# Early expert loads into regions that the mixers have left, and two modulation groups summed on VectorE, in a two-layer diffusion backbone

## What is computed

```python
# modulation: per layer six vectors, for the latent and the context stream
mod = silu(c) @ w_mod[l] + b_mod[l]            # w_mod (2, 1024, 6144)
# sub-layer 1: three token mixers, merged
y = g_a * (a @ w_br_mla) + g_b * (b @ w_br_na) + g_m * (m @ w_br_ml)
y = y @ w_out                                  # g_* = sigmoid of three 1024-wide slices of h @ w_in
# sub-layer 2: each of 16 experts takes its 32 best tokens of each stream
hid = silu(xs @ w1[e]) * (xs @ w3[e])          # w1, w3, w2: (2, 16, 1024, 1024)
y = (hid @ w2[e]) * g[e]                       # scattered back and added
```

## Time and profile before

| | us |
|---|---|
| median of 3 executions | 2017.98 |
| lowest, highest | 2014.64, 2026.0 |
| the profiled execution | 2019.38 |
| its span, first to last instruction | 2017.6 |
| TensorE busy (share of the span) | 1724.3 (85%) |
| VectorE busy | 456.9 (23%) |
| ScalarE busy | 325.8 (16%) |
| expert loads: 384 of 1 MB, median from issue to landing | 17.9 |
| mean granted clock of TensorE | 0.933 |

### The profile page before, as it was taken

One profiled execution on the slowest core, in us unless ns is written; L12 is line 12 of the kernel. 1 busy time (PEld: TensorE's weight loads), 2 busy tenths in 40 slices (PEclk: granted clock), 3 DMA queues, 4 the chain that ended last, 5 costly groups with the idle time before them and its releaser, 6 DMA issues.

```text
span 2017.6 us, 21841 instructions
## 1 busy us (share of the span) xinstructions
PE 1724.3 (85%) x9307; PEld 884.3 (44%) x9307; DVE 456.9 (23%) x990; ACT 325.8 (16%) x776; POOL 93.3 (5%) x168
## 2 busy tenths in 40 slices
PE   6999999999998998979888799999996666676665
PEld 2656354444476332424222376767873323222221
DVE  2045144211113112112120514253112101011102
ACT  4113243100023100101000311242021000000001
POOL 5000110000012000000000000110000000000000
PEclk9999999999999999999999899999997778777777
DMA  9310104545416999999999922114635999999995
GB/s 348 101 42 21 16 1 188 196 159 187 147 65 238 403 421 422 421 421 421 421 421 421 389 85 63 16 32 157 209 126 241 421 421 421 421 420 421 421 421 247
DMA packets 130668, 525.18 MB, mean 260 GB/s; under 512 B 9886, under 2 KB 73532, under 8 KB 75276
## 3 DMA queue, kind: packets, MB, share of 16 engines
q1 hardware_dynamic: 127884, 520.47, 65.3%
q0 software_dynamic: 2688, 3.32, 0.9%
HBM read 522.70 MB, written 1.05 MB: 260 GB/s over the span
## 4 chain that ended last, share of the span: by engine, by line
PE 57%; DMA 37%; DVE 4%; ACT 1%; issue 1%; SPq 0%; DVEq 0%; ACTq 0%
DMA ring<-in_w_e_dram 36%; PE ps L690 13%; PE ps L950 9%; PE ps L1127 6%; PE ps L956 4%; PE ps L986 4%; PE ps L914 3%; PE ps L876 2%; PE ps L619 2%; PE ps L1081 2%; PE ps L1149 2%; PE ps L792 2%; PE ps L1107 2%; PE ps L625 1%; DMA ring<-in_w_mod_dram 1%; PE ps L898 1%
## 5 line engine op out<-in xcount | busy, mean ns | idle before, releaser
L1127 PE MATMUL ps<-ring,arena 128*32 128x256 f32 (+1 forms) x3072 | 409.2, 512 | 129.4 <-DMA ring<-in_w_e_dram 126.5
L1127 PEld LDWEIGHTS ps<-ring,arena 128*32 128x32 f32 (+1 forms) x3072 | 131.7, 130 | 391.6 <-DMA ring<-in_w_e_dram 213.1
L1149 PE MATMUL ps<-ring,arena 128*32 128x256 f32 (+1 forms) x1536 | 221.5, 560 | 84.6 <-DMA ring<-in_w_e_dram 80.8
L950 PE MATMUL ps<-arena,ring 128*128 128x512 f32 (+1 forms) x576 | 192.4, 487 | 0.0
L690 PE MATMUL ps<-arena,ring 128*128 128x512 f32 (+1 forms) x480 | 176.9, 527 | 1.4 <-DVE arena L1671 1.4
L1149 PEld LDWEIGHTS ps<-ring,arena 128*32 128x32 f32 (+1 forms) x1536 | 70.5, 140 | 231.4 <-issue 114.7
L1495 ACT ACTIVATE arena<-ps 128x512 f32<-128x512 f32 (+1 forms) x32 | 15.7, 490 | 815.6 <-PE ps L1127 815.6
L950 PEld LDWEIGHTS ps<-arena,ring 128*128 128x128 f32 x576 | 108.7, 190 | 77.9 <-issue 70.4
L1890 DVE COPY arena<-ps 32x512 f32<-32x512 f32 (+1 forms) x128 | 70.8, 553 | 284.1 <-PE ps L1149 282.8
L690 PEld LDWEIGHTS ps<-arena,ring 128*128 128x128 f32 x480 | 90.8, 191 | 83.6 <-issue 77.7
L1195 ACT ACTIVATE arena<-ps 128x512 f32<-128x512 f32 (+4 forms) x162 | 78.4, 489 | 210.9 <-PE ps L986 65.8
(11 more groups left out here) (200 smaller groups left out, 1309.5 us busy)
## 6 DMA issues: line engine op xcount, KB each, us to landing
ring<-in_w_e_dram SPq DMA_DIRECT2D x384, 1024.0 KB, 17.9
ring<-in_w_mod_dram SPq DMA_DIRECT2D x48, 1024.0 KB, 9.2
ring<-in_w_in_dram SPq DMA_DIRECT2D x44, 1024.0 KB, 10.1
ring<-in_w_out_dram SPq DMA_DIRECT2D x8, 1024.0 KB, 10.2
arena<-in_w_br_ml_dram SPq DMA_DIRECT2D x8, 512.0 KB, 6.4
arena<-in_w_br_mla_dram SPq DMA_DIRECT2D x8, 256.0 KB, 3.8
arena<-in_w_br_na_dram SPq DMA_DIRECT2D x8, 256.0 KB, 4.7
arena<-in_rpb_dram POOLq DMA_DIRECT2D x16, 96.0 KB, 4.1
```

The source lines that it names most:

```text
L950: mm = pe.matmul(ps[:, u % 3, tq], wg[:, k, cols], hT[:, k, tq], start=k == 0, stop=k == KD - 1)
L1127: mm = pe.matmul(ps[M * j:M * j + M, m, 0:NW], XST[e // GROUP % 2][:, kk, e % GROUP, 0:M], w[:, k, j * NW:(j + 1) * NW], start=kk == 0, st ...
L1149: mm = pe.matmul(ps[M * j:M * j + M, 3, 0:NW], lhs, w[:, k, j * NW:(j + 1) * NW], start=kk == 0, stop=kk == KD - 1)
```

## The change

What it does:

- **Early expert loads.** `SPARE` names, by the place of a load in the expert order (from 0), loads that go to a region outside the ring. In layer 0 these are loads 0 to 3, into `mix0` to `mix3`, which are the first 8192 columns of the arena (the projections' input and the mixers' outputs). In layer 1 they are 0 (the rows of the context in `X`), 1 (`mixer_consts`: masks, rope table and a projection, now in one tensor), 2 (the first branch buffer), 7 to 10 (`mix0` to `mix3`) and 11 (the second half of `merged`). Each region has a condition that SP waits for (`spare_free`). Every region is used once in a layer; all other loads take the ring's slots in turn, and each waits for the load that had its slot before (`PREVIOUS`).
- **Order of issue.** In layer 0 SP issues expert loads 0 to 3 ahead of the last four modulation loads of group 4; in layer 1 expert loads 0 and 1 ahead of the four output weights.
- **Modulation.** In layer 0 group 1 is computed on TensorE in the first six units (three, three and two products). Groups 2 and 3 are summed on VectorE: after each unit from u = 6 and from u = 15, for eight units, `mod_part` takes one load and adds it, times the column of silu(c), to two sums of 128 x 2048 (`mod_acc`, one for each stream). TensorE sums these over the partitions at u = 14 and u = 23 (8 matmuls each, with `pick`, a column of ones), and releases the slots of these loads in order with its own, in each odd unit, ahead of the last two branch matmuls.
- **What had to move for it.** The gate rows of group 2 are spread in the round e = 14 in place of 1. Scratch areas for squares, the transposed rows, the gathered rows and the gates get other addresses; in layer 1 the memset of `Ya` covers the latent half.

The diff, cut to its core:

```diff
@@ -109,15 +108,18 @@
-def mod_steps(step):
-    n = 3 * KD
-    return range(n * step // MERGE_STEPS, n * (step + 1) // MERGE_STEPS)
-def mod_step(o):
-    return next(s for s in range(MERGE_STEPS) if o * KD - 1 in mod_steps(s))
+def mods_first(l, step):
+    return [(1, k) for k in range(3 * step, min(3 * step + 3, KD))] if l == 0 and step < 3 else []
+SUMMED = {2: 6, 3: 15}
+def mods_summed(l, u):
+    return [(o, u - first) for o, first in SUMMED.items() if l == 0 and first <= u < first + KD]
...
@@ -132,8 +134,10 @@
                 loads += [("in", layer, C_BG + m * D + jp * BLK, BLK)]
-            if layer == 0:
-                loads += [("mod", *MOD_GROUPS[1 + n // KD], n % KD) for n in mod_steps(3 * jp + m)]
+            step = 3 * jp + m
+            for u in (2 * step - 1, 2 * step):
+                loads += [("mod", *MOD_GROUPS[o], k) for o, k in mods_summed(layer, u)]
+            loads += [("mod", *MOD_GROUPS[o], k) for o, k in mods_first(layer, step)]
         if 1 <= jp < KD // 2 - 1:
...
@@ -192,6 +196,42 @@
+SPARE = [{0: "mix0", 1: "mix1", 2: "mix2", 3: "mix3"},
+         {0: "ctx_rows", 1: "mixer_consts", 2: "branch0", 7: "mix0", 8: "mix1", 9: "mix2", 10: "mix3", 11: "merged_end"}]
+SLOT_OF, PREVIOUS, USE = [], [], []
+def _assign_slots():
+    turn, last, count = 0, {}, {}
+    for l in range(2):
+        spare = [None] * len(ring_loads(l)) + [SPARE[l].get(j) for j in range(len(EXPERT_LOADS))]
+        for name in spare:
+            slot = name
+            if name is None:
+                slot, turn = turn % SLOTS, turn + 1
+            count[slot] = count.get(slot, 0) + 1
+            PREVIOUS.append(last.get(slot))
+            last[slot] = len(SLOT_OF)
+            SLOT_OF.append(slot)
+            USE.append(count[slot])
+_assign_slots()
+def issue_order(l):
+    order = [(w, None) for w in weight_loads(l)]
+    experts = [(("expert", l, *a), j) for j, a in enumerate(EXPERT_LOADS)]
+    if l == 0:
+        return order[:-4] + experts[:4] + order[-4:] + experts[4:]
+    return order[:-4] + experts[:2] + order[-4:] + experts[2:]
...
@@ -222,12 +262,13 @@
-        mask_f = sb("mask_f", 512)
-        mask_b = sb("mask_b", 640)
-        rope_t = sb("rope_t", 2, SEQ)
+        mixer_consts = sb("mixer_consts", 2176)
+        mask_f = mixer_consts[:, 0:512]
+        mask_b = mixer_consts[:, 512:1152]
+        wukv = mixer_consts[:, 1152:1664].rearrange("p (a n) -> p a n", a=2)
+        rope_t = mixer_consts[:, 1664:2176].rearrange("p (a n) -> p a n", a=2)
-        wukv = sb("wukv", 2, HEADS * 64)
...
@@ -272,7 +314,7 @@
-        junk1 = view(10240, D)
+        junk1 = view(19968, D)
...
@@ -296,22 +338,24 @@
+        mod_acc = [view(20992, SLOT), view(18432, SLOT)]
-        junk_y = view(0, D)
-        hot, Sr, Sg = (view(4096 + 512 * b, 2, 2, P) for b in range(3))
-        XT = view(8192, 4, KD, P)
-        XST = [view(8192 + 2048 * b, KD, GROUP, 64) for b in range(2)]
+        junk_y = view(12288, D)
+        hot, Sr, Sg = (view(19968 + 512 * b, 2, 2, P) for b in range(3))
+        XTs = [view(8192, 4, KD, P), view(6144, 4, KD, P)]
+        XSTs = [[view(8192 + 2048 * b, KD, GROUP, 64) for b in range(2)],
+                [view(8192 + 1024 * b, KD, GROUP, 32) for b in range(2)]]
-        G2 = view(19968, 2, D)
-        tmp2 = view(9216, D)
-        junk2 = view(8192, D)
+        G2s = [view(8192, 2, D), view(7168, 2, D)]
+        tmp2s = [view(10240, D), view(9216, D)]
+        junk2 = view(18432, D)
...
@@ -336,10 +380,17 @@
+        spare_slots = {**{f"mix{i}": view(SLOT * i, SLOT) for i in range(4)},
+                       "ctx_rows": X[:, 0:2, :].rearrange("p a d -> p (a d)"), "mixer_consts": mixer_consts[:, 0:SLOT],
+                       "branch0": view(14336, SLOT), "merged_end": view(10240, SLOT)}
         def w_slot(n):
-            return ring[:, n % SLOTS, :]
-        landed = [sem(f"weights_landed_{i}") for i in range(SLOTS)]
+            s = SLOT_OF[n]
+            return spare_slots[s] if isinstance(s, str) else ring[:, s, :]
+        def landed(n):
+            return sem(f"weights_landed_{SLOT_OF[n]}")
         used = sem("weights_used")
...
@@ -357,14 +408,31 @@
+            def spare_free(l, name):
+                if name[:3] == "mix" and name[3:].isdigit():
+                    sp.wait_ge(sem("mg_branch"), before("mg_branch", l) + 24)
+                elif name == "ctx_rows":
+                    sp.wait_ge(sem("n1_xn"), before("n1_xn", l) + 4)
+                elif name == "mixer_consts":
+                    sp.wait_ge(sem("roped"), before("roped", l) + 1)
+                    sp.wait_ge(sem("proj_ready"), pj_index(l, "v3") + 1)
+                elif name == "branch0":
+                    sp.wait_ge(sem("mg_branch"), before("mg_branch", l) + 18)
+                else:
+                    sp.wait_ge(sem("wo_ready"), before("wo_ready", l) + 4 * layers[l].nt)
             def load(n, dst, src):
-                if n >= SLOTS:
-                    sp.wait_ge(used, n - SLOTS + 1)
-                sp.dma_start(dst, src).then_inc(landed[n % SLOTS], 16)
+                if isinstance(SLOT_OF[n], str):
+                    spare_free(0 if n < BASE[1] else 1, SLOT_OF[n])
+                elif PREVIOUS[n] is not None:
+                    sp.wait_ge(used, PREVIOUS[n] + 1)
+                sp.dma_start(dst, src).then_inc(landed(n), 16)
             for l in range(2):
-                n = BASE[l]
-                for kind, lw, *a in weight_loads(l):
+                n_ring, n_expert = BASE[l], BASE[l] + len(ring_loads(l))
+                for (kind, lw, *a), j in issue_order(l):
+                    n = n_ring if j is None else n_expert + j
                     if kind == "branch":
...
@@ -382,14 +450,14 @@
-                    else:
+                    elif kind == "out":
-                    n += 1
-                for e, m, q in EXPERT_LOADS:
-                    w = (w_e1, w_e3, w_e2)[m][l, e].rearrange("(q p k) n -> q p (k n)", q=4, p=P)
-                    load(n, w_slot(n), w[q])
-                    n += 1
+                    else:
+                        e, m, q = a
+                        load(n, w_slot(n), (w_e1, w_e3, w_e2)[m][l, e].rearrange("(q p k) n -> q p (k n)", q=4, p=P)[q])
+                    if j is None:
+                        n_ring += 1
...
@@ -626,15 +697,34 @@
-            def merge_mods(step):
-                for n in mod_steps(step):
-                    o, k = 1 + n // KD, n % KD
-                    if k == 0:
+            def mods_done(l, u):
+                mods = mods_summed(l, u - 2) + mods_summed(l, u - 1)
+                if mods:
+                    o, k = mods[-1]
+                    pe.wait_ge(sem("mod_part"), KD * (o - 2) + k + 1)
+                taken[0] += len(mods)
+                return len(mods)
+            def merge_mods(u):
+                if u % 2:
+                    for o, k in mods_first(0, u // 2):
+                        if k == 0:
+                            pe.wait_ge(sem("mod_row"), o)
+                        mod_product(o, k)
+                if u == 7:
+                    mod_turn(1)
+                for o, first in SUMMED.items():
+                    if u == first + KD:
+                        pe.wait_ge(sem("mod_part"), KD * (o - 1))
                         pe.wait_ge(sem("mod_row"), o)
-                    mod_product(o, k)
-                for o in range(1, 4):
-                    if mod_step(o) == step - 1:
+                        for s in range(2):
+                            for j in range(4):
+                                mm = pe.matmul(ps[32 * j:32 * j + 32, 6, :], pick[:, s, :], mod_acc[s][:, 512 * j:512 * j + 512],
+                                               start=s == 0, stop=s == 1, skip_group_check=True)
+                        mm.then_inc(sem("mod_summed"), 1)
+                    if u == first + KD + 2:
...
@@ -952,15 +1042,18 @@
                             nk_ = 4 if m == 2 else 2
+                            freed = 0
                             for k in range(nk_):
+                                if k == nk_ - 2 and half:
+                                    freed = (1 if jp else 0) + mods_done(l, u)
                                 mm = pe.matmul(ps[:, 3 + u % 3, tq], wb[:, k0 + k, cols], src[:, k, tq],
                                                start=k == 0, stop=k == nk_ - 1)
-                                if k == 0 and jp and half:
-                                    mm.then_inc(used, 1)
+                                if freed and k == nk_ - 2:
+                                    mm.then_inc(used, freed)
                             mm.then_inc(sem("mg_branch"), 1)
+                            if l == 0:
+                                merge_mods(u)
                             u += 1
-                        if l == 0:
-                            merge_mods(3 * jp + m)
...
@@ -1067,8 +1160,6 @@
                 def gather(g):
```

(54 more changed lines are left out.)

23 lines of the change are left out of this document (10 added, 13 removed).

## The result

| | before | after |
|---|---|---|
| median (runs), us | 2021.99 (4) | 1984.72 (4) |
| lowest to highest | 2014.64 to 2028.55 | 1982.38 to 1991.88 |
| ratio, 95% interval | | 0.9827, 0.9801 to 0.9853 |
| profiled execution, span | 2019.38, 2017.6 | 1984.07, 1982.1 |

The changed kernel is 1.7% faster. The forecast was 1986.4 us. Between the two profiled executions the span fell by 35.5 us, where my sum said 31.6. The kernel before is in this table with one execution more (2028.55) than the forecast started from, which moves its median from 2017.98 to 2021.99.

What follows compares the result with a forecast made beforehand. TensorE was taken to bound the merge, and the start of the load stream with the MB left then the expert stages. Savings of 11.1 + 3.1 + 17.4 = 31.6 us against the median 2017.98 gave 1986.4 us, range 1980 to 1995.

Steps and rivals of the forecast that it cites:

- my sum: Whole kernel: 11.1 (merge) + 3.1 (layer 0) + 17.4 (layer 1) = 31.6 us saved.
- Merge: Layer 0's merge: 16 products leave TensorE (14.8 us), two sums are added (3.7 us), net -11.1 us.
- Layer 0: Layer 0's expert stage: 4 MB early save 10.0 us, the stream restarts 6.9 us later, net -3.1 us.
- the gap: Start of layer 0's expert stage: DMA idle about 9 us ahead of its restart, after TensorE's fifth load.
- Rival B: Expert stages: early MB count in full, 10.0 us in layer 0 and 20.1 in layer 1, 1976.8 us; chance 0.06.
- Layer 1: Layer 1's expert stage: 8 MB early save 20.1 us, the restart comes 2.7 us later, net -17.4 us.
- the lower clock of my bound: Layer 1's first loads: TensorE still at its lower clock, four loads take 7.1 us, saving only 13.9 us.
- C: Merge: VectorE streams 2048 columns at half rate, 4.5 us an operation, stalls up to 24 us, 2010.8 us; chance 0.06.
- D: Merge: VectorE becomes the bound outright; 31 us of stalls at 4.7 us an operation, 2031.6 us at 5.2; chance 0.03.
- my step: Merge, slow VectorE: stepping through the units, two take 22.5 us in place of 17.2 or 20.6.
- E: Expert stages: SP's order holds early loads until the ring's own, only the merge's part is left, 2006.9 us; chance 0.05.
- the moved gate rows: Layer 0, second to fifteenth expert: 8 instructions, 3.60 us, made up in seven more loads, before the tail.

Runs made afterwards that it cites:

- the repeat: The changed kernel run again with nothing altered, as the measure for the kernels beside it: 1985.74 us (5 runs), ratio 0.9836.
- the batching run: Against the kernel before, the modulation products on TensorE come by fours after every second pair of units: 2018.73 us (10 runs), ratio 0.9995.
- the two kernels that change only the order: Against the changed kernel, early loads are used behind the ring's eight: 1979.45 us; the same with layer 0's four spread over loads 16 to 34: 1979.22 us.
- the kernel with two early loads: Against the changed kernel, only two early loads ahead of the ring's in layer 0 and four behind them in layer 1: 1996.58 us, ratio 0.9887.
- three operations a load: Against the changed kernel, VectorE does one more 128x2048 operation per load, on a column of zeros: 1992.22 us, ratio 0.9869, merge 198.74 us.

## Why the prediction was right

**The time.** The sum was 31.6 us; the profiled executions lie 35.5 us apart, the medians 37.3, and 33.3 beside the repeat. So the sum was short in each of the three, by 1.7 to 5.7 us. That the forecast of 1986.4 lies only 1.7 us from the measured 1984.72 is in part luck: it started from a median of 2017.98 for the kernel before, which another execution moved to 2021.99. The mechanisms are judged by the stages.

**Merge.** Forecast -11.1 us, measured -12.7. VectorE's part was right to 3 ns, with no wait. The term that was mis-sized is TensorE's: "two take 1.85 us from their start to the next group's, so 0.925 each" (the rows have 1.86) holds neither the branch product made longer ahead nor the gate product behind, and it hides that 0.34 us at each place belongs to the place and not to the product. By the sizes of the batching run, before is 24 x 0.855 + 12 x 0.34 = 24.6 us; after is 8 x 0.855 + 3 x 0.34, and two sums at 1.71 + 0.34, 12.0 us. The difference is 12.6.

**Layer 0.** Forecast -3.1, measured -3.1 (-3.9 in the repeat). The exact figure is luck: the three rows of the table without early loads have 455.1 to 456.5 us, the five with the changed kernel's order 452.0 to 452.8, and the means differ by 3.7. What mattered was that 4 MB less are not 10 us less, as the ring behind the early loads stays full until the fifth has been used; the issue time, the gap, and the two kernels that change only the order show it. Rival B (each MB counts in full) would have this stage at 445.9 us, so it is refuted, and again by the kernel with two early loads. With the regions behind the ring's loads, though, its price is nearly what one gets: 447.0 to 448.3 us, and 446.2 spread out.

**Layer 1.** Forecast -17.4, measured -18.2; the delay is the expected one, and the 0.8 us over lie within what these stages vary by: the means of the same three and five rows (455.4 to 456.4 and 437.9 to 438.3) differ by 17.8. TensorE ran its first 20 loads without a wait at full clock (1.00 from 1515 on), where I had forecast sixteen; the lower clock of my bound did not come.

**Rivals C and D.** Neither came; the slope of the earlier trace rows holds at 2048 columns. The Trainium skill's rule (Vector Engine (DVE) Microarchitecture Reference, "Points that are easy to get wrong") that a scalar_tensor_tensor with two SBUF sources that aren't bf16 runs at half throughput would give 4.5 us here if the half is taken of the rate in the earlier trace rows; measured are 2.35, so in that sense it does not hold. Against an operation with one source from SBUF the trace agrees with it: the plain multiply takes 1367 ns for 2048 columns and 853 for 1024 (L1654), 0.50 ns a column to 1.04. D's price was too low: I let stalls of 31 us just eat the gain at 4.7 us an operation and put the loss only above that. At two more operations a load, the same VectorE time, the stalls are 31.7 us and the kernel is 0.5% slower than before. What my step left out is TensorE's clock, which fell at six of the eight waits; C was priced without it too.

**E and the moved gate rows.** The early loads were issued where the order has them, from 550.23 in layer 0 and by 1489.56 in layer 1, 25 us ahead of the first use at 1515.04. The spreading of the gate rows in the fifteenth expert left no mark: the 188th load is used as it lands. No run moves it back, since its old place in memory is taken by the change; its cost of nothing is argued and not shown.

## What to carry to other kernels

Memory added ahead of a stream that DMA bounds is worth what DMA moves early less the time for which it then stands still. Put the early loads behind those of the ring in order of use, so that the first use lets a slot go at once; here that was worth a further 6 us of the median (1985.74 to 1979.45) for another order in two tables, with no byte more. And look for the longest run of uses that free nothing: if DMA's queue is shorter than that, DMA goes short of loads. Spreading them closed that hole, but what it gained here (0.8 to 2.2 us of the stage) did not show in the time.

Work moved from a full engine to an idle one is free as long as each piece ends before the next point at which the full engine asks for it. That is to be checked piece by piece, not by totals: with three operations a load VectorE was busy 137 of the merge's 199 us, and TensorE waited all the same.

## What was not expected of the hardware

- Small products between large ones on TensorE cost 0.34 us for each change, on top of 0.855 us a product (8 instructions of 128x512 into four column groups): the group ahead is 0.09 us longer, the one behind 0.10, the products 0.15.
- A wait of 5.07 us in a stretch in which TensorE is otherwise busy was followed by 5.4 us at half the granted clock (0.50, the level of 1.2 GHz), so that it cost 7.8 us: 1.8 more in the branch product and 0.9 in the gate product behind it. Of the eight waits of that kernel before branch products, those of 5.07, 2.51, 5.54, 2.39, 5.04 and 5.30 us went with such a fall, those of 1.25 and 2.96 us did not, nor did the four of the kernel with three operations (0.98 to 1.84 us). So the length of a wait alone does not tell.
